# The first query slab ahead of the norm's sum, and sixteen peer slabs outside the loop, six of them among the query slabs

## What is computed

```python
def peer_ffn(h, w_query, keys1, keys2, expert_u, expert_v):
    q = (hf @ w_query).reshape(t, PEER_HEADS, 2, PEER_HALF)
    s1 = jnp.einsum('thc,hnc->thn', q[:, :, 0], keys1)
    s2 = jnp.einsum('thc,hnc->thn', q[:, :, 1], keys2)
    v1, i1 = lax.top_k(s1, PEER_TOPK)
    v2, i2 = lax.top_k(s2, PEER_TOPK)
    cand_s = (v1[..., :, None] + v2[..., None, :]).reshape(t, PEER_HEADS, PEER_TOPK * PEER_TOPK)
    top_s, top_pos = lax.top_k(cand_s, PEER_TOPK)
    gate = jax.nn.softmax(top_s.astype(jnp.float32), axis=-1).astype(h.dtype)
    ...
    act = jax.nn.gelu(jnp.einsum('thk,td->thk', expert_u[ib], hb), approximate=False)
    return jnp.einsum('thk,thkd->td', gb * act, expert_v[ib])
```

## Time and profile before

| | |
|---|---|
| median of 3 runs | 2159.47 us (2158.83 to 2160.36) |
| the profiled execution: its time, its span | 2158.3 us, 2156.5 us |
| TensorE busy (matmuls) | 2049.1 us, 95% of the span |
| VectorE busy | 1448.2 us, 67% |
| ScalarE busy | 1062.1 us, 49% |
| GpSimd busy | 63.8 us, 3% |
| DMA over the span | 353.60 MB, mean 164 GB/s |

### The profile page before, as it was taken

The page is one execution under the profiler, slowest core; times in us unless marked ns, Lnnn a source line. Parts: engine busy times, 40 slices in busy tenths (PEclk is TensorE's granted clock), DMA queues, the critical chain, the costliest instruction groups (busy, mean ns, idle before and its releaser), DMA issues.

```text
span 2156.5 us, 41022 instructions
## 1 busy us (share of the span) xinstructions
PE 2049.1 (95%) x15332; PEld 1949.2 (90%) x15332; DVE 1448.2 (67%) x2353; ACT 1062.1 (49%) x1640; POOL 63.8 (3%) x40
## 2 busy tenths in 40 slices
PE   7899889999999999999989998799999999999997
PEld 7899888999999999999879998789999999889997
DVE  5787698876666666666776556675556556856555
ACT  5445435864444444444455444554445444545443
POOL 0000260000000000000000000000000000000000
PEclk9999999999999999999999999999999999999999
DMA  5344443235555555555665554245555555435553
GB/s 193 128 137 146 149 137 116 76 112 184 187 186 185 191 183 188 186 184 192 199 203 182 185 184 157 87 153 185 179 178 173 175 185 166 138 128 176 185 184 99
DMA packets 101456, 353.60 MB, mean 164 GB/s; under 512 B 11392, under 2 KB 16640, under 8 KB 101120
## 3 DMA queue, kind: packets, MB, share of 16 engines
q1 hardware_dynamic: 100944, 350.13, 50.3%
q10 hardware_dynamic: 432, 2.36, 0.3%
HBM read 348.77 MB, written 3.67 MB: 163 GB/s over the span
## 4 chain that ended last, share of the span: by engine, by line
PE 85%; DVE 10%; ACT 4%; issue 1%; DMA 0%; SPq 0%; DVEq 0%; ACTq 0%
PE front L1759 38%; PE acc L1759 32%; PE tile L1759 14%; DVE w_lo L1065 1%; ACT w_hi L665 1%; DVE rstd L1088 1%; DVE h_lo L1095 1%; DVE cand L1440 0%; DVE x L1590 0%; DVE rest L1409 0%; DVE top_i L1405 0%; DVE top_i L1423 0%; DVE top_v L1401 0%; ACT G L847 0%; DVE orr L1353 0%
## 5 line engine op out<-in xcount | busy, mean ns | idle before, releaser
L1065 DVE TENSOR_TENSOR w_lo<-raw,w_hi 128x1024 fp32r<-128x1024 f32 x616 | 753.7, 1224 | 174.8 <-ACT w_hi L665 174.5
L665 ACT CAST w_hi<-raw 128x1024 fp32r<-128x1024 f32 x632 | 659.8, 1044 | 347.1 <-PE front L1759 143.9
L1759 PE MATMUL front<-h_hi,w_hi 128*128 128x256 f32 x2272 | 644.9, 284 | 8.5 <-DVE h_lo L1095 7.1
L1759 PE MATMUL front<-h_hi,w_lo 128*128 128x256 f32 x2272 | 643.5, 283 | 0.0
L1759 PE MATMUL front<-h_lo,w_hi 128*128 128x256 f32 x2272 | 643.5, 283 | 0.0
L1759 PEld LDWEIGHTS front<-h_hi,w_hi 128*128 128x128 f32 x2272 | 436.2, 192 | 14.6 <-DVE h_lo L1095 5.3
L1759 PEld LDWEIGHTS front<-h_lo,w_hi 128*128 128x128 f32 x2272 | 436.3, 192 | 4.2
L1759 PEld LDWEIGHTS front<-h_hi,w_lo 128*128 128x128 f32 x2272 | 436.3, 192 | 0.0
L714 ACT ACTIVATE scaled<-scaled 128x256 f32<-128x256 f32 x196 | 81.9, 418 | 459.1 <-DVE scaled L1150 247.4
L1145 DVE TENSOR_TENSOR scaled<-front,rstd 128x512 f32<-128x512 f32 x88 | 60.8, 691 | 275.5 <-PE front L1759 275.4
L1759 PE MATMUL tile<-h_hi,w_hi 128*128 128x256 f32 x736 | 219.1, 298 | 22.8 <-DVE h_lo L1208 4.9
(11 more groups left out here) (269 smaller groups left out, 2769.7 us busy)
## 6 DMA issues: line engine op xcount, KB each, us to landing
raw<-stream SPq DMA_DIRECT2D x632, 512.0 KB, 3.6
early_u<-stream SPq DMA_DIRECT2D x20, 512.0 KB, 3.6
early_activations<-early_out SPq DMA_DIRECT2D x20, 128.0 KB, 3.5
scaled<-early_activations SPq DMA_DIRECT2D x10, 128.0 KB, 3.8
x<-x_t SPq DMA_DIRECT2D x2, 512.0 KB, 4.6
keysT<-keys_t ACTq DMA_DIRECT2D x1, 1024.0 KB, 5.5
attc<-attention_constants ACTq DMA_DIRECT2D x1, 1024.0 KB, 5.4
out_t<-h SPq DMA_DIRECT2D x4, 256.0 KB, 2.2
```

Source lines behind the costliest of these rows:

```text
L665: nc.scalar.copy(w_hi[:, s, :], raw[:, s, :]).then_inc(hi_ready, 1)
L1065: nc.vector.tensor_tensor(w_lo[:, s, :], raw[:, s, :], w_hi[:, s, :].bitcast(F32), ALU.subtract).then_inc(lo_ready, 1)
L1759: return nc.tensor.matmul(out, lhsT, rhs, start=start, stop=stop, **kw)
```

## The change

- The number of early slabs falls from 20 to 16; the peer loop takes 112 steps. Slabs 0 to 5 stand among the query slabs, behind slabs 5, 7, 9, 11, 13 and 15 (counted from 0), slabs 6 and 7 in the choice, one block to a mask, and slabs 8 to 15 over the gate table, with 1.5 blocks to a step for 43 steps.
- The first query slab no longer stands behind the norm's sum: `norm(1)` follows the second query slab and writes to another bank. ScalarE's root stands behind its copy of the second slab, VectorE's reciprocal behind the first ranking, the transposes of rstd behind the fifth slab, the copy of the columns ahead of the fifth ranking.
- GpSimd makes `h_scaled` in eight instructions of two tiles each, two behind the low half of each of the fifth to the eighth query slab. The first early slab waits for all eight.
- SyncE issues the first four early loads ahead of the loads of the query slabs, and the later early loads and stores among them.

```diff
@@ -114,8 +114,10 @@
-EARLY, U_BUFFERS = 20, 4
+EARLY, U_BUFFERS = 16, 4
 EARLY_IN_CHOICE = 8
+EARLY_AT = {5: 0, 7: 1, 9: 2, 11: 3, 13: 4, 15: 5}
 LOOP_STEPS = NKEYS - EARLY
@@ -505,10 +507,11 @@
+        sum_at[1] = banks[:, 2, 0:T]
+
+        def early_blocks(at):
+            return range(3 * at // 2, min(3 * (at + 1) // 2, KT * (EARLY - EARLY_IN_CHOICE)))
@@ -564,15 +567,26 @@ SyncE
-            steady(RING, first["peer"] + RING)
-            sp.wait_ge(slab_used, first["branch"] + 1)
-            for j in range(U_BUFFERS):
-                load_early(j)
-            for j in range(EARLY):
+            def store_early(j):
                 if j + U_BUFFERS < EARLY:
                     load_early(j + U_BUFFERS)
                 sp.wait_ge(early_ready, j + 1)
                 sp.dma_start(early_dram[j, :, :], early_out[:, j % 2, :]).then_inc(early_stored[j % 2], 16)
+            n = first["wquery"]
+            steady(RING, n)
+            sp.wait_ge(slab_used, first["branch"] + 1)
+            for j in range(U_BUFFERS):
+                load_early(j)
+            steady(n, n + 2 * RING)
+            for i in range(16):
+                if n + i + 2 * RING < first["peer"] + RING:
+                    load(n + i + 2 * RING)
+                if i in EARLY_AT:
+                    store_early(EARLY_AT[i])
+            for j in range(len(EARLY_AT), EARLY):
+                store_early(j)
             sp.wait_ge(pick_used, T)
@@ -614,22 +628,22 @@ GpSimd
                     for n in range(first["wquery"] + RING, first["peer"] + RING):
-                        if n == first["wquery"] + 3 * RING:
-                            pool.wait_ge(rstd_ready, 2)
-                            for step, k in enumerate((0, 4, 0, 4)):
...
                         pool.wait_ge(lo_ready, n)
                         pool.wait_ge(hi_ready, n + 1)
                         nc.gpsimd.tensor_tensor(w_lo[:, n % RING, :], raw[:, n % RING, :],
...
+                        k = 2 * (n - first["wquery"] - RING)
+                        if k < KT:
+                            g = cols[:, COL["norm_ffn_g"] + k:COL["norm_ffn_g"] + k + 2]
+                            pool.wait_ge(rstd_ready, 2)
+                            nc.gpsimd.tensor_tensor(h_scaled[:, k:k + 2, :], x[:, k:k + 2, :],
+                                                    rstd[:, :].unsqueeze(1).broadcast_to([P, 2, T]),
+                                                    ALU.mult).then_inc(h_scaled_steps, 1)
+                            pool.wait_ge(h_scaled_steps, k + 1)
+                            nc.gpsimd.tensor_tensor(h_scaled[:, k:k + 2, :], h_scaled[:, k:k + 2, :],
+                                                    g.unsqueeze(2).broadcast_to([P, 2, T]),
+                                                    ALU.mult).then_inc(h_scaled_steps, 1)
@@ -811,11 +825,8 @@ ScalarE
                 split_hi(late)
-                root(1)
                 n = first["wquery"]
-                for i in range(16):
-                    take("wquery", i, qT[:, i, :])
-                    split_hi(n + i + RING)
...
-                for j in range(EARLY_IN_CHOICE - 3):
-                    early_gelu(j)
+                for i in range(16):
+                    take("wquery", i, qT[:, i, :])
+                    if i == 1:
+                        root(1)
+                        split_hi(n + RING)
+                    if i >= 1:
+                        split_hi(n + i + RING)
+                    if i in EARLY_AT:
+                        early_gelu(EARLY_AT[i])
                 act.wait_ge(gate_diff, 1)
                 nc.scalar.activation(gts[:, :, :, :], gts[:, :, :, :], ACT.Exp).then_inc(gate_exp, 1)
-                for j in range(EARLY_IN_CHOICE - 3, EARLY_IN_CHOICE):
+                for j in range(len(EARLY_AT), EARLY_IN_CHOICE):
                     early_gelu(j)
@@ -851,7 +869,7 @@
-                    if turn == EARLY - EARLY_IN_CHOICE + 1:
+                    if turn == T // 16 - 3:
...
-                    if turn < EARLY - EARLY_IN_CHOICE:
-                        early_gelu(EARLY_IN_CHOICE + turn)
+                        for of in early_blocks(turn * 4 + b):
+                            if of % KT == KT - 1:
+                                early_gelu(EARLY_IN_CHOICE + of // KT)
@@ -1099,7 +1118,8 @@ VectorE
-                nc.vector.tensor_copy(r_col[:, :], front[:, 1, 0:T:P]).then_inc(r_col_ready, 1)
+                to = banks[:, 3, 0:T:P] if count == 1 else front[:, 1, 0:T:P]
+                nc.vector.tensor_copy(r_col[:, :], to).then_inc(r_col_ready, 1)
@@ -1384,7 +1404,8 @@
-                inverse_rms(1, late)
+                add_squares(1)
+                split_lo(late)
@@ -1450,10 +1471,13 @@
-                    if i == 1:
+                    if i == 5:
                         r_columns(1)
                     if i >= 1:
                         placed = best_keys(i - 1)
+                    if i == 1:
+                        dve.wait_ge(roots, 2)
+                        nc.vector.reciprocal(rstd[:, :], rstd[:, :]).then_inc(rstd_ready, 1)
@@ -1821,8 +1845,9 @@ TensorE
+                to = banks[:, 3, :] if q < 2 else front[:, 1, :]
                 for tt in range(TT):
-                    ins = nc.tensor.transpose(front[:, 1, tt * P:(tt + 1) * P], rstd[:, tt * P:(tt + 1) * P],
+                    ins = nc.tensor.transpose(to[:, tt * P:(tt + 1) * P], rstd[:, tt * P:(tt + 1) * P],
@@ -2005,7 +2030,9 @@
                         if j == 0:
-                            pe.wait_ge(h_scaled_steps, 4)
+                            pe.wait_ge(h_scaled_steps, KT)
+                        if j == 3:
+                            pe.wait_ge(r_col_ready, 1)
@@ -2014,16 +2041,11 @@
-                norm(1)
-                pe.wait_ge(keys_in_sem, 16)
...
-                    if i == 1:
-                        pe.wait_ge(r_col_ready, 1)
@@ -2033,14 +2055,16 @@
                 for i in range(16):
                     project("wquery", i, n + i, h_hi, h_lo, 8 if i == 0 else None)
-                    if i == 0:
+                    if i == 1:
+                        norm(1)
+                        pe.wait_ge(keys_in_sem, 16)
+                    if i == 4:
                         turn_rstd(1)
                     if i >= 1:
                         key_scores(i - 1)
-                early_scores(0, range(KT))
+                    if i in EARLY_AT:
+                        early_scores(EARLY_AT[i], range(KT))
                 key_scores(15)
-                for j in range(1, EARLY_IN_CHOICE - 3):
-                    early_scores(j, range(KT))
@@ -2051,8 +2075,7 @@
-                    for of in range(3 * a // 2, 3 * (a + 1) // 2):
-                        early_scores(EARLY_IN_CHOICE - 3 + of // KT, [of % KT])
+                    early_scores(len(EARLY_AT) + a // KT, [a % KT])
@@ -2078,11 +2101,11 @@
-                        late_turn = turn - (EARLY - EARLY_IN_CHOICE)
-                        if late_turn < 0:
-                            early_scores(EARLY_IN_CHOICE + turn, range(2 * b, 2 * b + 2))
-                        elif 1 <= 4 * late_turn + b <= KT:
-                            seed_x(4 * late_turn + b - 1)
+                        for of in early_blocks(turn * 4 + b):
+                            early_scores(EARLY_IN_CHOICE + of // KT, [of % KT])
+                        m = turn * 4 + b - T // 4 + 16
+                        if 1 <= m <= KT:
+                            seed_x(m - 1)
```

## The result

The changed kernel takes **2161.86 us**, median of 12 runs (2161.44 to 2166.5), the kernel before 2159.43 us in 12 runs (2157.86 to 2160.36): a ratio of 1.0018, 95% interval 1.001 to 1.0026. That is 2.4 us, inside the 0.2% that a measurement of this kernel tells from no change; the forecast was 2163.6. The runs of the changed kernel fall in two groups, seven at 2161.4 to 2162.1 and five at 2165.3 to 2166.5. The profiled execution is one of the upper group: 2165.73 us, span 2163.9.

A forecast was written before the change was run, and what follows sets the result against it. TensorE bounds the kernel nearly throughout, except mainly where VectorE's ranking sets the pace (259 to 335 us). Choice +4.1, gate table -11.5, peer loop +11.5 sum to +4.1 us: 2163.6 us, own range 2162.0 to 2165.2, wider range 2158.8 to 2167.2.

The forecast's parts named there:

- Start: Ahead of the query slabs: norm follows the second slab without a wait; first key scores at 250.95 us against about 259.0.
- rival (c): ScalarE's table load stands in the path at the start: +5.5 us, 2165.0 us, slower; chance 0.05.
- h_scaled: GpSimd's eight steps among the query slabs end at about 271.7 us, leaving TensorE 6.6 us idle before early slab 0.
- Rival (a): Before early slab 0: GpSimd is done before TensorE arrives, no wait; -1.0 us, 2158.5 us; chance 0.12.
- Query slabs: Pairs with an early slab take 10.08 us against VectorE's 7.94, so TensorE is the bound; ranking ends 5.0 us later.
- rival (e): Among query slabs TensorE keeps up and VectorE's head start holds: 2150 to 2156 us, faster; chance 0.07.
- Clock: Lower TensorE clock loses 2.3 us behind the wait before early slab 0 and 2.5 us in the choice.
- Rival (b): Clock returns later behind early slab 0 and in the choice; at 3.6 us each +6.5 us, 2166.0 us; chance 0.13.
- SyncE's loads: First four early loads, ahead of the query slabs' loads, fit a gap and cost nothing; without it up to 5 us.
- rival (d): Early loads stall the last output slabs or first query slabs: up to +5 us on top, 2168 us; chance 0.03.
- Table and loop: Gate table shorter by 11.5 us; peer loop longer by 11.5 us for four slabs that change sides.

The follow-up runs named there:

- start: Changed kernel with early slabs placed and numbered as before, so only the new start and GpSimd's eight spread steps remain: 2153.4 us, ratio 0.9976.
- late: Changed kernel with each of the first five early slabs further back, behind query slabs 7, 9, 11, 13, 14: 2156.15 us, ratio 0.9994.
- twenty: Changed kernel with 20 early slabs again, 12 over the gate table at two blocks a step, 108 loop steps: 2166.29 us, ratio 1.0028.
- again: Changed kernel with no edit, run once more with its own profile: 2166.19 us, ratio 1.0027.
- mix: Changed kernel with one early block behind each of query slabs 8 to 15 and five early slabs behind the last key scores: 2150.75 us, ratio 0.9963.
- mix2: Changed kernel with two early blocks behind each of query slabs 8 to 15 and four early slabs behind the last key scores: 2149.98 us, ratio 0.9957.
- again2: Changed kernel with no edit, a third time, for a profile of its lower group: one run, 2163.16 us.

## Why the prediction was right, point by point

- **Start.** The first query slab begins with the low halves, the norm follows the second slab, no low clock before 260: as predicted. GpSimd's first low half starts 10.12 us behind h, predicted 10.06. The table load is 1.28 us and the root starts 1.29 behind its beginning: no drain in the trace, which speaks against the figure of about 1.38 us in the Trainium skill (ScalarE: Activation LUTs, What ACT_TABLE_LOAD costs) and against rival (c). The reciprocal beside GpSimd takes 1.73 us, 1.75 before, so this instruction, which has one input, is indeed not stretched, while the two sums, which have two, take 3.11 (0.46 undisturbed).
- **h_scaled.** A step of low half and two scalings takes 4.7 to 4.8 us, predicted 4.54, since the half-size pair is 1.29 + 1.04 and not 2.15. The eighth ends 29.05 us behind h instead of 28.3. The idle time is 6.77 us, predicted 6.6. Rival (a) is out.
- **Query slabs.** Pairs of 10.08 us to the hundredth, so TensorE is the bound and GpSimd's hold on VectorE costs nothing. Last ranking sum 92.41 us behind h, predicted 92.3: rival (e) is out; start shows that VectorE's head start does hold where the early slabs stand elsewhere.
- **Clock.** Early slab 0 and the query slab behind it take 281.13 - 273.15 = 7.98 us, where 3.46 + 2.87 = 6.33 was their due: 1.65 us lost, predicted 2.3. The choice takes 354.00 - 340.74 = 13.26 for 11.45: 1.8 lost, predicted 2.5. Both were oversized, by 1.35 us together; the later eighth step of h_scaled takes some 0.75 of that back, and this leaves about the 0.5 us between +3.6 and +4.1. The 1.7 us that the prediction read behind 4.32 us of idle is nearer 1.6: that slab with its scores took 296.50 - 291.63 = 4.87 us instead of 3.31. Rival (b), at 3.6 each, is out.
- **SyncE's loads** caused no stall (rival (d)): no engine waits for a load from 200 us to h, the stretch that I feared for. Whether the 0.56 us by which h itself is later comes from them is not shown: h is 244.4 and 245.0 in the other two profiles of this kernel, but 242.0 in late, with the same loads, and the kernel before has one profile only.
- **Table and loop.** -11.46 and +11.5, confirmed by twenty. The prediction's sum for the table before takes 1.76 us a step where it had read 1.75; with 1.75 it gives -11.0.
- **What the sum did not hold** is the second block, 3.1 us more in the profiled execution and 3.1 in again's; that it is so in the other runs of the upper group is inferred from their times. The sum was +4.1 and its stages gave +3.65. The rest of every difference of times, down to +2.4 for the median and up to +6 to +7 for the upper group, lies outside the change's own steps; how it divides is known only for the profiled execution.

The forecast held, then, by its own steps: a cost of about 4 us, at the places and for the reasons that it gives. That the time fell so near to 2163.6 is in part luck. The median, 2161.86, lies 0.1 below the forecast's own range of 2162.0 to 2165.2, because seven of the twelve runs were of the lower group; the same kernel as again, with six of ten in the upper one, had 2166.19, 1.0 above that range.

The small sum hides two large terms of opposite sign: 8 us gained at the start, and more than that given back from slab 5 on, by the pairs of 10.08 us and by the wait for h_scaled (late and start tell them apart). The step where I could have seen more is the choice of place: the pair of 7.94 us for VectorE against 6.6 for TensorE leaves 0.66 us a slab, room for one block and not for four.

## What to carry to other kernels

A head start gained on one engine lives only as long as no work put behind it exceeds the gap between the two engines' paces; lay filler in portions near that gap (here one block of 0.43 us a slab, or two, which overrun it by little) and only from the point where its operands are surely there. Moving equal work between two stages with the same bound was worth nothing here, which twenty shows to 0.2 us. Compare stages from a fixed instruction, not the totals: here the untouched second half moved by 3.1 us, nearly as much as the change's own 3.65.

## What the runs showed of the hardware that was not expected

- **The same short wait costs clock in one kernel and not in the next.** Ahead of the gate table TensorE waits 2.57 us for VectorE in all ten profiles. Busy times by stretch there, first mix, then mix2:

```profile
345.00:347.00 2.00, 1.39 (x8) 1.42 (x9) 2.00 (x5) 1.71 (x6) 0.00 (x0) 0.74 0.57 213
347.00:349.00 2.00, 2.00 (x9) 1.82 (x9) 2.00 (x6) 1.31 (x5) 0.00 (x0) 0.50 0.02 4
```

```profile
346.00:348.00 2.00, 1.04 (x9) 1.07 (x10) 2.00 (x5) 1.36 (x5) 0.00 (x0) 1.00 0.74 270
348.00:350.00 2.00, 2.00 (x15) 1.80 (x15) 2.00 (x6) 1.59 (x6) 0.00 (x0) 1.00 0.02 4
```

  In mix 9 of TensorE's records fall into the second stretch at 0.50, in mix2 15 at 1.00. late is like mix2 at the table (first scaling 99.1 us behind the choice), the changed kernel like mix in what it costs (100.8). First the changed kernel, then late, the same products of the table's first steps:

```profile
358.40 1.92 PE L1783 MATMUL front<-picks_mid 128*128 128x128 f32 x8
```

```profile
352.28 1.05 PE L1783 MATMUL front<-picks_mid 128*128 128x128 f32 x8
```

  In mix2 and late the engine had waited and run at the lower clock in the choice, some 12 us earlier, and in mix it had not. But that does not decide it: the changed kernel had done so too, behind its 11.47 us. What does is open.

- **A wait of 2.56 us can be enough.** In late, behind the 2.56 us before early slab 0 (columns as in the earlier trace rows):

```profile
274.00:276.00 2.00, 1.43 (x6) 1.37 (x7) 2.00 (x15) 1.84 (x2) 1.96 (x1) 0.52 0.70 236
276.00:278.00 2.00, 2.00 (x7) 1.68 (x6) 1.97 (x13) 0.49 (x1) 1.96 (x1) 0.63 0.60 166
```

  So can 2.04 us, ahead of the choice in mix2:

```profile
332.00:334.00 2.00, 2.00 (x11) 1.54 (x9) 2.00 (x5) 0.39 (x1) 0.00 (x0) 0.50 0.20 64
```

  The length of a wait alone did not tell what it cost: 1.6 us lost behind 2.04 (mix2, 13.04 us for 11.45), 1.65 behind 6.77, 1.8 behind 11.47, 1.6 behind 4.32 before.

- **Times of one kernel in two groups** 4 to 5 us apart, on one core. 2.9 us of that are seen in the profiles, in a stage that the change does not touch, and go with the clock granted there, 0.91 against 0.95 over 100 us (again, again2).
